# Attention scores from stacked query parts: four full-array products per unit in place of three pairs of half-array products

## The reference, cut to what matters

```python
q = rope(q.reshape(bsz, s, N_HEADS, HEAD_DIM), positions)
k_sel = rope(heads(k_sel), positions)
k_win = rope(heads(k_win), positions)
...
sc = jnp.einsum('bqhgd,bhqkd->bhgqk', qb, kg, preferred_element_type=f32) * scale
p = masked_softmax(sc, m_sel)
...
sc = jnp.einsum('bqhgd,bkhd->bhgqk', qb, kw, preferred_element_type=f32) * scale
p = masked_softmax(sc, m_win)
```

## Time and profile before

| | |
|---|---|
| median of 3 runs | 1749.88 us (1749.79 to 1750.62) |
| the profiled execution's own time | 1750.73 us |
| its span in the trace | 1748.6 us |
| TensorE busy (share of the span) | 1725.9 us (99%) |
| VectorE busy | 944.3 us (54%) |
| ScalarE busy | 649.2 us (37%) |
| GpSimd busy | 119.4 us (7%) |
| mean granted TensorE clock | 0.999 |
| chain that ended last, by engine | PE 89%, DVE 5%, DVEq 2%, ACT 1%, DMA 1% |

### The profile page before, as it was taken

One profiled execution on the slowest core, in us unless ns is written; L12 is line 12 of the kernel. 1 busy time (PEld: TensorE's weight loads), 2 busy tenths in 40 slices (PEclk: granted clock), 3 DMA queues, 4 the chain that ended last, 5 costly groups with the idle time before them and its releaser, 6 DMA issues.

```text
span 1748.6 us, 26744 instructions
## 1 busy us (share of the span) xinstructions
PE 1725.9 (99%) x10172; PEld 1406.7 (80%) x10172; DVE 944.3 (54%) x1520; ACT 649.2 (37%) x1146; POOL 119.4 (7%) x241
## 2 busy tenths in 40 slices
PE   7999999999999999999999999999999999999998
PEld 7788777788888888888888877777888888888886
DVE  5888777554364444422359877864453644444223
ACT  4334666422242222221343346664222422222112
POOL 5700000000000000000055000000000000000000
PEclk9999999999999999999999999999999999999999
DMA  8443111122522222222374431112233222222222
GB/s 268 152 119 89 55 50 48 61 97 99 168 85 85 97 97 97 99 94 93 109 235 122 107 88 55 43 49 72 97 118 111 85 96 96 96 96 96 97 96 84
DMA packets 67646, 174.88 MB, mean 100 GB/s; under 512 B 14448, under 2 KB 26768, under 8 KB 67296
## 3 DMA queue, kind: packets, MB, share of 16 engines
q1 hardware_dynamic: 43072, 151.01, 25.1%
q10 hardware_dynamic: 21888, 13.64, 3.3%
q0 software_dynamic: 2592, 8.92, 1.7%
HBM read 162.27 MB, written 7.08 MB: 97 GB/s over the span
## 4 chain that ended last, share of the span: by engine, by line
PE 89%; DVE 5%; DVEq 2%; ACT 1%; DMA 1%; issue 1%; SPq 0%; ACTq 0%
PE ps L537 19%; PE ps L539 19%; PE ps L538 19%; PE ps L580 5%; PE ps L579 5%; PE ps L578 5%; PE ps L883 2%; PE ps L870 2%; PE ps L856 2%; DMA raw<-wstream 1%; PE ps L558 1%; PE ps L569 1%; PE ps L560 1%; PE ps L559 1%; PE ps L859 1%
## 5 line engine op out<-in xcount | busy, mean ns | idle before, releaser
L537 PE MATMUL ps<-xh,whi 128*128 128x512 f32 x1312 | 519.6, 396 | 2.5 <-ACT gates L1237 2.4
L539 PE MATMUL ps<-xh,wlo 128*128 128x512 f32 x1312 | 511.4, 390 | 0.0
L538 PE MATMUL ps<-xl,whi 128*128 128x512 f32 x1312 | 510.8, 389 | 0.0
L1425 DVE TENSOR_TENSOR wlo<-raw,whi 128x1024 fp32r<-128x1024 f32 x254 | 313.2, 1233 | 324.9 <-ACT whi L1003 319.0
L1003 ACT ACTIVATE whi<-raw 128x1024 fp32r<-128x1024 f32 x248 | 262.5, 1059 | 332.3 <-PE ps L580 216.6
L537 PEld LDWEIGHTS ps<-xh,whi 128*128 128x128 f32 x1312 | 246.4, 188 | 53.1 <-issue 3.6
L539 PEld LDWEIGHTS ps<-xh,wlo 128*128 128x128 f32 x1312 | 246.2, 188 | 52.4
L538 PEld LDWEIGHTS ps<-xl,whi 128*128 128x128 f32 x1312 | 246.6, 188 | 48.9 <-issue 0.5
L578 PE MATMUL ps<-whi,hh 128*128 128x512 f32 x336 | 131.3, 391 | 0.0
L580 PE MATMUL ps<-whi,hl 128*128 128x512 f32 x336 | 130.8, 389 | 0.0
L579 PE MATMUL ps<-wlo,hh 128*128 128x512 f32 x336 | 130.7, 389 | 0.0
(11 more groups left out here) (357 smaller groups left out, 2385.0 us busy)
## 6 DMA issues: line engine op xcount, KB each, us to landing
raw<-wstream SPq DMA_DIRECT2D x264, 512.0 KB, 3.2
w<-w1s SPq DMA_DIRECT2D x16, 512.0 KB, 7.2
sm<-smalls POOLq DMA_DIRECT2D x2, 1060.0 KB, 6.4
xt<-xin ACTq DMA_DIRECT2D x4, 512.0 KB, 6.4
scratch_u<-pa ACTq DMA_DIRECT2D x8, 256.0 KB
toep<-scratch_k ACTq DMA_DIRECT2D x4, 512.0 KB
toep_b<-scratch_k ACTq DMA_DIRECT2D x4, 512.0 KB
xt<-xin POOLq DMA_DIRECT2D x4, 512.0 KB, 4.2
```

The source lines that it names most:

```text
L537: pe.matmul(ps[:, bank, :], wh, hi[:, k, :], start=first and i == 0, stop=False)
L538: pe.matmul(ps[:, bank, :], wh, lo[:, k, :], start=False, stop=False)
L539: m = pe.matmul(ps[:, bank, :], wl, hi[:, k, :], start=False, stop=last and i == len(blocks) - 1)
L1425: dve.tensor_tensor(wlo[:, c % 2, :], raw[:, c % 2, :], whi[:, c % 2, :].bitcast(f32), SUB).then_inc(lo_ready, 1)
```

## The change

Each key head's query gets a full-height operand: for key head 0 the high part in partitions 0 to 63 and the low part in 64 to 127, for key head 1 the other way round (`q_parts[j][v]`). The keys' high part and low part of each key head stand on both halves (`k_high[v]`, `k_low[v]`). DVE writes one half of each; GpSimd issues four transfers of 256 KB between halves (`keys_in`), and PE waits for them ahead of the first unit of a layer. `scores` then makes four products of 128 rows: stacked query times high keys and times low keys, for each key head. This adds low times low to the sum, which the six products left out. `key_parts`, and the two halves of the former `query_parts`, run as two instructions of 64 partitions each in place of one of 128; the low part is written to the other half. `query_low` runs at u = 5, `gelu_low` moves from u = 5 to u = 6. `prob` goes from three slots to two, and buffers change places.

```diff
@@ small parameters: order
-               ("cim", GP * SC), ("dsk", SG), ("psc", 4), ("b1", 4), ("wg", KD * 32), ("wpool", 4 * P),
-               ("w2", 4 * HD), ("pos", 2 * SC)):
+               ("cim", GP * SC), ("psc", 4), ("b1", 4), ("wpool", 4 * P), ("wg", KD * 32),
+               ("w2", 4 * HD), ("pos", 2 * SC), ("dsk", SG)):
...
-    prob = more("prob", [P, 3, 2, S])
+    prob = more("prob", [P, 2, 2, S])
     probt = more("probt", [P, 2, 2, S])
+    kh_b = place("kh_b", at, [P, 2, S], f32r)
+    at += 2 * S
...
+    q_parts = ((q_a0, q_b0), (q_a1, q_b1[0]), (q_a0, q_b0), (q_a1, q_b1[1]))
+    kh_a = place("kh_a", used["sm"][0] + SM["bre"][0], [P, 2, S], f32r)
+    kl_a = place("kl_a", used["kro"][0], [P, 2, S], f32r)
+    kl_b = place("kl_b", used["sm"][0] + SM["wg"][0], [P, 2, S], f32r)
+    k_high, k_low = (kh_a, kh_b), (kl_a, kl_b)
...
@@ GpSimd, behind eph_ready and ahead of shift_q(1)
+                wait(keys_split, l + 1)
+                for k in (k_high, k_low):
+                    pool.dma_start(k[0][HD:P, :, :], k[0][0:HD, :, :]).then_inc(keys_in, 16)
+                    pool.dma_start(k[1][0:HD, :, :], k[1][HD:P, :, :]).then_inc(keys_in, 16)
...
@@ TensorE, scores
-                    qh, ql = qhis[i // 8], qlos[i // 8]
-                    for a, b in ((qh, krh), (ql, krh), (qh, krl)):
-                        for kv in range(2):
-                            rows = slice(64 * kv, 64 * kv + 64)
-                            pe.matmul(ps[:, sbank(i) + kv, 0:n], a[rows, P * t:P * t + P], b[rows, br, 0:n],
-                                      start=a is qh and b is krh, stop=False)
+                    for kv in range(2):
+                        q = q_parts[i // 8][kv]
+                        for k in (k_high[kv], k_low[kv]):
+                            pe.matmul(ps[:, sbank(i) + kv, 0:n], q[:, P * t:P * t + P], k[:, br, 0:n], start=k is k_high[kv], stop=False)
...
                 pe.wait_ge(masks_ready, 2)
+                pe.wait_ge(keys_in, (l + 1) * 64)
                 pe.wait_ge(q_ready, l * 4 + 2)
                 compressed_scores(0, 3)
...
@@ VectorE, key_parts
-                    dve.tensor_copy(krh[:, :, :], kro[:, :, :])
-                    dve.drain()
-                    tt(krl[:, :, :], kro[:, :, :], krh[:, :, :].bitcast(f32), SUB)
+                    for v in range(2):
+                        rows = slice(HD * v, HD * v + HD)
+                        dve.tensor_copy(k_high[v][rows, :, :], kro[rows, :, :])
+                    dve.drain()
+                    for v in range(2):
+                        rows = slice(HD * v, HD * v + HD)
+                        x = tt(k_low[v][rows, :, :], kro[rows, :, :], k_high[v][rows, :, :].bitcast(f32), SUB)
+                    x.then_inc(keys_split, 1)
...
-                def query_parts(j):
+                def query_high(j):
                     q, q_shift, _ = att_bufs(j)
                     dve.drain()
                     tt(q[:, :], qt1[:, :], q_shift[:, :], ADD)
                     dve.drain()
-                    dve.tensor_copy(qhis[j][:, :], q[:, :])
-                    dve.drain()
-                    tt(qlos[j][:, :], q[:, :], qhis[j][:, :].bitcast(f32), SUB).then_inc(q_ready, 1)
+                    for v in range(2):
+                        rows = slice(HD * v, HD * v + HD)
+                        dve.tensor_copy(q_parts[j][v][rows, :], q[rows, :])
+
+                def query_low(j):
+                    q = att_bufs(j)[0]
+                    dve.drain()
+                    for v in range(2):
+                        rows, other = slice(HD * v, HD * v + HD), slice(HD - HD * v, P - HD * v)
+                        x = tt(q_parts[j][v][other, :], q[rows, :], q_parts[j][v][rows, :].bitcast(f32), SUB)
+                    x.then_inc(q_ready, 1)
...
                     if u == 4 and j < 3:
-                        query_parts(j + 1)
-                    if u == 5:
+                        query_high(j + 1)
+                    if u == 5 and j < 3:
+                        query_low(j + 1)
+                    if u == 6:
                         gelu_low(j)
```

More of the change, by code:

```diff
@@ L141, in build_program @@
     toep = own("toep", [P, 8, P])
-    sm = own("sm", [P, NSM])
     nrm = own("nrm", [P, L, 32])
@@ L151, in build_program @@
     dmaskb = own("dmaskb", [P, P], mybir.dt.bfloat16)
+    sm = own("sm", [P, NSM])
     pa = place("pa", big_at + 8192, [P, 10, S])
@@ L169, in build_program @@
     st = more("st", [P, 16, GP])
+    at = big_at + 17408
     u8_c = more("u8_c", [P, 8, NCH])
@@ L227, in build_program @@
     qraws = (qraw_a, qraw_b)
[L228 to L234, removed]
+    q_a0 = place("q_a0", big_at + 19200, [P, S], f32r)
+    q_b0 = place("q_b0", big_at + 19712, [P, S], f32r)
+    q_a1 = place("q_a1", used["nsh"][0] + 3 * S, [P, S], f32r)
+    q_b1 = [place("q_b1_%d" % n, used["nsl"][0] + n * S, [P, S], f32r) for n in (2, 3)]
+    q_parts = ((q_a0, q_b0), (q_a1, q_b1[0]), (q_a0, q_b0), (q_a1, q_b1[1]))
[3 more added lines that the diff above has]
+    k_high, k_low = (kh_a, kh_b), (kl_a, kl_b)
     qt1 = place("qt1", used["toep"][0] + S, [P, S])
@@ L292, in build_program @@
         qrot_psum, q_shifted, q_ready = sem("qrot_psum"), sem("q_shifted"), sem("q_ready")
+        keys_split, keys_in = sem("keys_split"), sem("keys_in")
         cs_psum, cs_taken, cs_shift, cs_exp, cs_ready, cs_tpsum, cs_tready = (
@@ L869, in turned @@
                             bank, at = turned_at(i, kv)
-                            m = pe.transpose(ps[:, bank, at + P * k:at + P * k + P], prob[:, i % 3, kv, P * k:P * k + P], ident)
+                            m = pe.transpose(ps[:, bank, at + P * k:at + P * k + P], prob[:, i % 2, kv, P * k:P * k + P], ident)
                     m.then_inc(s_tpsum, 1)
@@ L1301, in exps @@
                     for kv in range(2):
-                        x = act.activation(prob[:, i % 3, kv, 0:n], ps[:, sbank(i) + kv, 0:n], ACT.Exp,
+                        x = act.activation(prob[:, i % 2, kv, 0:n], ps[:, sbank(i) + kv, 0:n], ACT.Exp,
                                            bias=tiny[:, 28 + 8 * (i % 3) + kv:29 + 8 * (i % 3) + kv],
@@ L1309, in scale @@
                     act.wait_ge(s_ratio, l * 32 + (i + 1))
-                    act.activation(prob[:, i % 3, 0, 0:n], prob[:, i % 3, 0, 0:n], ACT.Copy, scale=tiny[:, 52 + 2 * (i % 3):53 + 2 * (i % 3)])\
+                    act.activation(prob[:, i % 2, 0, 0:n], prob[:, i % 2, 0, 0:n], ACT.Copy, scale=tiny[:, 52 + 2 * (i % 3):53 + 2 * (i % 3)])\
                        .then_inc(p_first, 1)
@@ L1865, in scale @@
                     dve.drain()
-                    dve.tensor_scalar(prob[:, i % 3, 1, 0:n], prob[:, i % 3, 1, 0:n], rat[:, 1:2], None, MUL).then_inc(p_second, 1)
+                    dve.tensor_scalar(prob[:, i % 2, 1, 0:n], prob[:, i % 2, 1, 0:n], rat[:, 1:2], None, MUL).then_inc(p_second, 1)
                 def heads_low(j):
@@ L1890, in _ @@
                 rope(0)
-                query_parts(0)
+                query_high(0)
+                query_low(0)
                 scan(l * 4 + 3, 3)
```

## The result

The changed kernel takes 1769.95 us (median of 4 runs, 1769.36 to 1770.58), the kernel before 1749.84 us beside it: ratio 1.0111, 95% interval 1.0099 to 1.0123. It is slower by 20.1 us, where the prediction had 5.0 and a range up to 1760.5. The profiled execution took 1769.91 us, 19.2 over that of before; its mean granted TensorE clock is 0.992 (0.999 before). That small difference turns out to matter.

A forecast was written before the change was run, and what follows sets the result against it. PE, busy 99% of the span, was taken as the bound. Terms -7.8 + 0.5 + 4.9 + 8.4 - 1.0 = +5.0 us on the profiled 1750.73 gave 1755.7, as a median 1754.9 us; range 1747 to 1760.5.

The forecast's parts named there:

- Its sign: Whole kernel: the change makes it slower, +5.0 us on the profiled execution; chance of slower by 0.2% 0.56.
- the keys' transfers: Layer start: four transfers between halves land at 159.5 to 163.6, hidden behind PE's wait at the first `turned`; cost 0.
- The units on PE: Scores: four full-array passes replace three pairs, saving 0.49 us per unit of each length, -7.8 us; +0.5 lost at starts.
- The mask's change of type: bfloat16 mask behind fp32r scores: taken as zero; rival keeps 0.09 us in each of 64 units, 1760.7, chance 0.07.
- The rival of the half-array passes: Scores on PE: half-array passes use the array better and edges don't shrink; +22.4 us, 1772.3; chance 0.03.
- The halves held on DVE: DVE's split instructions: the second 64 partitions cost a full duration and wait for the first; 0.70 per 512-column subtraction.
- DVE's later start: Start of a layer's stage: longer key and query parts delay the first `turned` by 2.45 us a layer, +4.9 us.
- keys late: Rival at the layer start: keys land at 166, not 163.4, adding 2.6 us a layer; 1760.1; chance 0.10.
- The cover: Layer start: PE waits at the first `turned` until 171.2 anyway, hiding 2.7 us of key lateness, up to 163.4.
- The six waits for the next pair's query: PE at u = 6, pair changes: low part comes late, stalls 1.0, 1.0 and 2.2 us a layer, +8.4 us.
- The term of 0.16 us for waking PE and a weight load: Pair changes: 0.16 us added between DVE's last query subtraction and PE's start, within each query stall.
- The probability copy's 1.0 us given back: Behind the stall at pair 2, PE no longer waits for a late probability copy: -1.0 us.

The follow-up runs named there:

- experiment 2: Changed kernel without the four key transfers and PE's wait for them, both key heads reading the same buffers: 1760.62 us.
- experiment 6: Kernel before, with DVE's key and query parts each made in two instructions of 64 partitions: 1760.97 us.
- experiment 1: Changed kernel plus four unread products into an unused bank on PE, just ahead of its wait for the keys: 1764.66 us.
- experiment 5: Kernel before plus the four key transfers, into buffers nobody reads, and PE's wait for them: 1762.34 us.
- experiment 3: Changed kernel with the next pair's low query part back at u = 4, directly behind the high part: 1759.93 us.
- experiment 7: Changed kernel with low query parts at u = 4 and slab 11's products ahead of the wait for the keys: 1753.95 us.
- experiment 10: Kernel before with slab 11's products ahead of the first scores and the last S5 outputs ahead of the first `turned`: 1752.81 us.

## Why the prediction was wrong, step by step

Its sign was right; the size was not, and the result lies 9 us over the range. The step that failed is the one on the keys' transfers, put at 0: they cost some 10 us in the two layers, 2.8 as lateness and 7.3 through the granted clock, and experiment 2 gives 9.3 back without them. The clock, which no term of the sum had, also took 3.0 behind the waits ahead of pair 3.

- **The units on PE: right.** -0.49 for one of each length was forecast, and the medians give 0.175 + 0.17 + 0.105 + 0.044 = 0.49 saved. The sum agrees better than its parts (0.13, 0.17, 0.13 and 0.06), whose errors cancel. The mask's change of type costs nothing, as taken. The rival of the half-array passes falls by the same rows: pairs of halves run side by side, but changing between shapes costs more than the fourth pass adds. Its 1772.3 is the number nearest to the result, and for another reason. The table's -6.1 leaves out the first unit of each new pair.
- **The halves held on DVE: right**, by the rows of the keys in the trace after and by experiment 6.
- **DVE's later start: right.** 2.45 us a layer forecast, 2.6 and 2.4 in experiment 2.
- **The keys' transfers at 0: this step failed.** Two sizes were off, and both made the landing late. GpSimd's drain and 1x1 instruction were put at 0.3 us and took 1.2, because they met the slab's subtraction on DVE; the trace of before had such a meeting at 1.23. The upper bound of 8.2 us came from two transfers of 512 KB in sequence, from memory; four of 256 KB within SBUF took 9.0, each 6.0 to 7.4, beside the slab's 512 KB and 512 KB of an S5 kernel; the prediction had named the transfers of both and costed them at nothing. Its own rule, "each us of lateness past 163.4 is one us a layer", was sound: landing at 164.85 makes 1.45, and without the clock's 3.9 the first `turned` would come at 172.4, 1.2 past the forecast 171.2. By it the sum was 7 to 8 and the forecast 1757 to 1758, half way to the rival "keys late" at 1760.1, whose mechanism held, and inside the range. So late keys alone don't explain the miss. The Trainium skill has a fit for one such transfer (DMA: Bandwidth & Descriptors, Anatomy of one DMA — SWDGE (gpsimd) path): 2.0 us and the bytes at 436 GB/s, an estimate of 2.6 us for 256 KB. No transfer here came near it.
- **The cover counted only time: the omission.** The prediction reckoned a wait as hidden if PE would have waited later anyway. It never asked what 4.7 us without work do to the granted clock. Experiments 1 and 5 show that they cost about as much again: 7.3 us at the two starts by the rows, 6.7 by experiment 1, and at pair 3 of each layer 3.4 us at half rate, about 1.5 lost each (the table's steps give 1.4). Together some 10 us, half of the 20.1 and two thirds of the error; without them the time would lie at about 1760, inside the range. Of layer 0's 4.7 us all but about 1.1 were covered (the prediction had 2.7 of cover, and PE asked 0.5 sooner), and the clock's 3.9 came on top. What a wholly covered wait costs no run here shows.
- **The six waits for the next pair's query: right.** 8.4 us forecast, 9.0 measured (1.2, 1.2 and 2.3 in layer 0 against 1.0, 1.0 and 2.2), in the places named; experiment 3 removes them. The term of 0.16 us for waking PE and a weight load had no row behind it; PE starts 0.05 to 0.06 us after DVE's last subtraction. The wait ahead of pair 3 brought the clock with it, which was not forecast.
- **The probability copy's 1.0 us given back: right**; that row is gone.

Put together with measured sizes, both layers: DVE's start 2.6 + 2.4, clock at the starts 3.9 + 3.4, keys 1.1 + 1.7 (not measured apart: what remains of the first `turned`'s 7.6 and 7.5), the six waits 9.0, clock behind pair 3's 3.0, copies -1.0, units -7.3 (-7.8 + 0.5). That is 18.8 against the 19.2 of the trace; I leave the remaining 0.4 open.

## What to carry to other kernels

Where TensorE bounds a kernel, read each wait that a change adds twice: for its length, and for the granted clock behind it; a wait of some microseconds can cost as much again. Existing work that does not depend on what the wait is for belongs in that place: here two blocks moved there, with the low part's step moved too, turned 20 us lost into 3.7 gained. A part computed for a later step should stand ahead of independent bulk work on its engine's queue, not behind it, and an engine busy for half of the span need not have 1 us free at the place where it is wanted.

## What the runs showed of the hardware that I had not expected

- The granted clock fell to 1.2 GHz behind all six waits of 2.7 to 4.7 us for the keys (the changed kernel, experiments 3 and 5) for 6.8 or 10.2 us. Waits of 1.8 to 2.5 us brought it down for 3.4 to 6.8 us in some layers and not in others of the same kernel: experiment 7's wait of 2.5 us in layer 0 only, experiment 6's in layer 1 only. The gate's wait of 1.41 us did so in experiment 10 and not in experiment 5. What decides between them stays open; it wasn't tried.
- A trace is one execution, and the clock differs between executions of the same kernel. Of 55 executions of the kernel before, run beside the experiments, six have a mean granted clock of 0.997 and took 1752.1 to 1753.9 us; the other 49 lie at 0.998 or above and took 1749.6 to 1751.8. Its one trace (0.999) has no stretch at 1.2 GHz in the attention stages; those six may have had one, which no trace shows.
- GpSimd's 1x1 instruction took 1.22 and 1.10 us beside a subtraction on DVE with both inputs in SBUF, ending 0.05 us after it, and 0.18 beside a DVE instruction with an input in PSUM (435.10 in the trace of before) or beside none.
- Four transfers within SBUF of 256 KB, issued from GpSimd's queue over 1.6 us, took 6.0 to 7.4 us each. How much of it is the slab's and the S5 kernel's transfers at the same time was not tried apart.
